# Delta rule scan: Grams of keys copied to SBUF once per chunk, kept in DRAM and loaded for the second visit

## The chip, the core and the metric

The kernel runs on one core of one Trainium2 chip. The metric is the device time of one execution in microseconds (us). The core has TensorE (PE, with its weight loads PEld), VectorE (DVE), ScalarE (ACT), GpSimd (POOL) and SyncE (SP), which here issues the DMAs. Matmuls write PSUM, eight banks of 128 x 512 fp32; the other operands are in SBUF.

## The reference

The program computes two transformer blocks on 512 tokens of width 1024, all in fp32: differential attention, a gated delta rule in both directions, an expert-choice feed-forward of 16 experts, and then a second block. The change touches the delta rule of the first block, which has 8 heads with keys and values of width 128 and runs once over the tokens and once over the reversed tokens. In each chunk, with keys k, a log decay g and a step beta, it needs (shortened):

```
k_beta = k * beta
a_mat  = where(strict, einsum('id,jd->ij', k_beta, k) * decay, 0)   # the Gram of keys, weighted
sol    = triangular_solve(a_mat + I, [v * beta, k_beta * exp(g)])
qk     = where(incl, einsum('id,jd->ij', q, k) * decay, 0)
# over the chunks:
v_new = u - w @ state
o     = q_dec @ state + qk @ v_new
state = state * g_last + k_dec.T @ v_new
```

The Gram of keys, k k^T of one chunk and head, depends on the keys alone. The decay and beta with which it is weighted are those of the direction.

## The kernel before

The stage works with chunks of 128 tokens (NT = 4 chunks) and walks through eight *positions*: `PAIRS[n] = (s, hg)`, step s = 0 to 3, and group of heads hg = 0 or 1. At a position both directions work at once, each on four heads: direction d = 0 on chunk s, direction d = 1 on chunk 3 - s. So a chunk that one direction meets in steps 0 and 1 is met by the other in steps 3 and 2: each Gram of keys is needed twice, once at positions 0 to 3 and once at positions 4 to 7. A position takes some 27 to 30 us.

The order of work on each engine is written out by hand: each engine has a loop over n with helper functions, and they meet by semaphores. While TensorE solves position n and runs the scan of n - 1, the others prepare n + 1. What matters for the change, by function and line of the profile:

- `gram_k` (L1246, TensorE): for each direction four matmuls 128 x 128 into the bank `bank(d, 1)`. In the trace an fp32 matmul shows as two records. In the loop it stands between `widest_P` (L1302) and `widest_X` (L1310) of the position before. `gram_q` (L1255) does the same for queries.
- `exponents` (L1591, L1592, VectorE), `decays` (L1427, L1432, ScalarE) and `keys` (L1487, GpSimd) make the factor BR of decay, mask and beta.
- `products` (VectorE): AT = Gram x BR, two instructions on L1598, then two on L1601 for the queries. Behind them stands `diagonal`: four small transposes on L1619 and one on L1611 (the semaphore `xop`).
- `level_P` (L1268, TensorE): the first matmuls of position n. They need AT of both directions and `xop`. Before the first position they need the inverses of 32 x 32 blocks too, which VectorE solves (L1651, L1653), and which go through DRAM: three stores to yrow (L1180) and four loads X32 (L1189).
- `corner` (L1643), `joined_T` (L1635), `outputs` (L1563), `states` (L1575) and `right` (L1584, L1586) are VectorE's other work in a position; `scan_ks` (L1327), `scan_v` (L1339), `scan_o` (L1349, L1351), `scan_s` (L1359) are TensorE's; L1219 is a filler, a projection of 8 matmuls 128 x 512 put where TensorE would wait, and ScalarE takes each out of PSUM (L1422).
- SyncE's one queue issues in its written order: pieces of weights for the fillers (L1157, 512 KB each, waiting until the filler two before is done), broadcast rows (L1166, L1173) and the transfers of inverses.

The place AT of direction d is the last but one (d = 0) or last (d = 1) eighth of the slab SL[2]; the scratch `sub` of the block solve is the same memory as AT of d = 1.

Of the kernel before, what the change touches and what calls it, by code (L numbers as in the profile page):

```python
# [13 lines left out]
F32 = mybir.dt.float32  # L14
ALU = mybir.AluOpType
# [3 lines left out]
P = 128  # L19
# [91 lines left out]
def build(nc, io):  # L111
    ctx = ExitStack()
    counts = {}
    with ctx:
# [5 lines left out]
        def sem(name):  # L120

            return cleared.pop(0) if cleared else ctx.enter_context(nc.semaphore(name))
# [667 lines left out]
        with nc.Block() as block:  # L790
# [200 lines left out]
            def _(dve):  # L991
# [28 lines left out]
                for p in range(NC3 + 1):  # L1020
# [46 lines left out]
        OG = SL[3][:, :]  # L1067
        ogT = OG.rearrange("p (h s) -> p h s", h=HEADS)
        names = ("zero", "lt_ready", "y_ready", "y_out", "x32", "xd_act", "xd_dve", "xop", "x64",
                 "gk_done", "gq_done", "row_read", "diff_ready", "qe_ready", "dec_ready", "ba_ready", "qd_ready", "AT_ready", "qk_ready",  # L1070
                 "P_done", "P_ready", "XO_done", "XO_ready", "XOT_done", "XOT_ready", "wP_done", "wP_ready", "XX_done", "XL_ready",
                 "ks_done", "bv_ready", "rr_ready", "vn_done", "vn_ready", "vs_ready", "o_done", "s_done",
                 "o_ready", "S_ready", "qq4", "sq4", "ss4", "rstd4", "og_ready", "ex_done", "ex_out", "ex_dve")
        E4 = {n: sem("d_" + n) for n in names}
        row_in = [sem(f"row_in{d}") for d in range(2)]
        brow_in = [sem(f"brow_in{d}") for d in range(2)]
        PAIRS = [(s, hg) for s in range(NT) for hg in range(2)]

        def all4(ap):
# [49 lines left out]
        def goes_on(n):  # L1129

            return PAIRS[n][0] < NT - 1

        def fresh(n):

# [8 lines left out]
        with nc.Block() as block:  # L1143
            @block.sync
            def _(sp):
# [48 lines left out]
                for m in range(3, KD + 2):  # L1194
                    load_piece(m)
                    if m in (5, 7, 8):
                        inverses_out((5, 7, 8).index(m))
                inverses_in()
                for m in range(KD, KD + AHEAD):
                    load_piece(m + 2)  # L1200
                rows(1)
                for n in range(len(PAIRS)):
                    if 1 <= n < len(PAIRS) - 1:
                        rows(n + 1)
                    for i in range(2):
                        m = extra(n, i)
                        if m is not None and m + 2 < len(EXTRA):
                            load_piece(m + 2)
                sp.wait_ge(E4["s_done"], 2 * (len(PAIRS) - 2))
                load_slab(sp, 7, w_in[:, GATE_G:GATE_G + 512], 512)  # L1210

            @block.tensor
            def _(pe):
# [26 lines left out]
                def gram_k(n):  # L1240
                    for q, d, c, heads, B, W in each(n):
                        if n:
                            pe.wait_ge(E4["AT_ready"], q - 1)
                        for i, h in enumerate(heads):
                            kc = gk[:, h, c * P:(c + 1) * P]
                            m = pe.matmul(part(bank(d, 1), i), kc, kc, start=True, stop=True)  # L1246
                        m.then_inc(E4["gk_done"], 1)
# [121 lines left out]
                for n in range(len(PAIRS) + 1):  # L1369
                    now, scan, ahead = n < len(PAIRS), n >= 1, n + 1 < len(PAIRS)  # L1370
                    if scan:
                        scan_ks(n - 1)
                    if now:
                        level_P(n)
                    if ahead:
                        gram_q(n + 1)
                    if now:
                        level_X(n)
                    if scan and now:
                        scan_v(n - 1)  # L1380
                    more(n, 0)
                    if now:
                        level_XT(n)
                    if scan and not now:
                        scan_v(n - 1)
                    if scan:
                        scan_o(n - 1)
                    if now:
                        widest_P(n)
                    if ahead:  # L1390
                        gram_k(n + 1)
                    if now:
                        widest_X(n)
                    if scan and goes_on(n - 1):
                        scan_s(n - 1)
                    more(n, 1)

            @block.scalar
            def _(act):
# [24 lines left out]
                def decays(n):  # L1424
# [5 lines left out]
                    for q, d, c, heads, B, W in each(n):  # L1430
                        act.wait_ge(E4["o_done"], q - 3)
                        a(cp(W["QD"], B["RW"], ACT.Exp), E4["dec_ready"])  # L1432

                def diagonal(n):

                    for q, d, c, heads, B, W in each(n):
# [17 lines left out]
                for m in range(1, KD - 1):  # L1454
                    attended(m)
                decays(0)
                attended(KD - 1)
                diagonal(0)
                filled(KD)
                for n in range(len(PAIRS) + 1):  # L1460
# [11 lines left out]
                        a(cp(flat(PMw), PS[0][:, 0:256], ACT.Copy), E4["wP_ready"])  # L1472
                    if ahead:
                        decays(n + 1)
                        diagonal(n + 1)
                    more(n, 1)

# [59 lines left out]
            def _(dve):  # L1537
# [56 lines left out]
                def products(n):  # L1594
                    for q, d, c, heads, B, W in each(n):
                        dve.wait_ge(E4["ba_ready"], q + 1)
                        dve.wait_ge(E4["gk_done"], q + 1)
                        v(tt(B["AT"], f4(bank(d, 1)[:, :]), B["BR"], ALU.mult), E4["AT_ready"])  # L1598
                    for q, d, c, heads, B, W in each(n):
                        dve.wait_ge(E4["gq_done"], q + 1)  # L1600
                        v(tt(W["QK"], f4(bank(d, 2)[:, :]), W["QK"], ALU.mult), E4["qk_ready"])  # L1601
# [181 lines left out]
            def expert_slab(eng, r):  # L1783
# [18 lines left out]
                for k in range(4):  # L1802
# [1 line left out]
                    slab_n[4 + k] += 16  # L1804
                    quarter_in.append((slab_in[4 + k], slab_n[4 + k]))

            spent.extend([inv["fac"], inv["rows"], inv["kt"], *piece_in, first_done, *row_in, *brow_in,
                          *[E4[n] for n in E4 if n not in ("qq4", "sq4", "ss4", "rstd4", "og_ready")]])
            @block.sync
            def _(sp):  # L1810
# [1588 lines left out]
```

## Time and profile before

| | us |
|---|---|
| runs, median (lowest to highest of 3) | 2232.25 (2231.83 to 2233.06) |
| profiled execution, its own time | 2233.42 |
| its span, first to last instruction | 2231.5 |
| TensorE busy | 2074.7 (93%) |
| VectorE busy | 905.9 (41%) |
| ScalarE busy | 484.1 (22%) |
| GpSimd busy | 230.2 (10%) |
| DMA moved | 499.98 MB |
| the stage of the change | from 463 to 755 in the span |

The span is what the trace shows; the execution's own time has 1.9 us more around it. An engine's share of busy time is a mean over stages with different limits, so each stage is read by itself. Columns of a timeline are the start in the span, the duration, the engine, the line, the operation, what it writes and reads, and in brackets how long the engine stood idle before and what ended that.

### The profile page before, as it was taken

What the parts mean: (1) busy time and instruction counts of PE and PEld (TensorE: products, weight loads), DVE (VectorE), ACT (ScalarE), POOL (GpSimd) and SP (SyncE); (2) the same over time, 40 slices, a digit from 0 to 9 for tenths busy, and PEclk for the clock granted to TensorE, in tenths of its full rate; (3) what the DMA queues carried; (4) which work ended last, traced back from release to release, by engine and by line L of the source; (5) the groups of instructions that cost most, each with busy time, mean ns of one, the idle gap of its engine ahead of it and who ended that gap; (6) DMA issues with size and microseconds to landing.
All of it is one profiled execution on the core that took longest, in us unless ns stands there. A gap on an engine that the chain in (4) does not pass through costs nothing.

```text
span 2231.5 us, 25322 instructions
## 1 busy us (share of the span) xinstructions
PE 2074.7 (93%) x10317; PEld 1130.4 (51%) x10317; DVE 905.9 (41%) x1507; ACT 484.1 (22%) x884; POOL 230.2 (10%) x163
## 2 busy tenths in 40 slices
PE   8999999998999999799999898989898978999998
PEld 5885564445666786443333333333332325865444
DVE  2447757783566653401110110101010104796964
ACT  2445645421222410100000000000000002332323
POOL 1320000301334030000000000000000003222000
PEclk9999999999999999899999999999999999999999
DMA  7220110024322334299999999999999996211111
GB/s 261 76 91 26 38 38 21 23 83 109 89 61 90 127 114 198 114 371 427 429 428 427 428 427 428 427 428 428 427 427 428 429 428 246 97 60 49 70 57 38
DMA packets 112789, 499.98 MB, mean 224 GB/s; under 512 B 23525, under 2 KB 51203, under 8 KB 87459
## 3 DMA queue, kind: packets, MB, share of 16 engines
q1 hardware_dynamic: 112675, 498.38, 55.8%
q8 instruction: 82, 1.34, 0.2%
q14 instruction: 32, 0.26, 0.0%
HBM read 493.31 MB, written 5.05 MB: 223 GB/s over the span
## 4 chain that ended last, share of the span: by engine, by line
PE 55%; DMA 19%; DVE 2%; ACT 1%; issue 1%; SPq 0%; DVEq 0%; ACTq 0%
PE PS L2059 8%; PE PS L2030 8%; DMA SL<-w_up 8%; PE PS L1219 7%; DMA R<-w_up 6%; PE PS L1919 4%; PE PS L2763 4%; PE PS L2740 3%; DMA SL<-w_down 3%; PE PS L1943 2%; PE PS L2004 2%; DMA SL<-w_gate 2%; PE PS L2759 1%; PE PS L3230 1%; PE PS L3224 1%; PE PS L2097 1%
## 5 line engine op out<-in xcount | busy, mean ns | idle before, releaser
L2030 PE MATMUL PS<-R 128*64 128x512 f32 x1024 | 230.4, 597 | 33.1 <-DMA R<-w_up 24.1
L2030 PE MATMUL PS<-SL,R 128*64 128x512 f32 x1024 | 227.2, 595 | 26.2 <-DMA SL<-w_gate 18.7
L2344 DVE TENSOR_TENSOR HT<-HT,PS 128x512 f32<-128x512 f32 x32 | 20.6, 684 | 365.2 <-PE PS L2030 365.2
L2030 PEld LDWEIGHTS PS<-SL,R 128*64 128x64 f32 x1024 | 72.5, 137 | 178.2 <-issue 128.2
L2030 PEld LDWEIGHTS PS<-R 128*64 128x64 f32 x1024 | 69.9, 137 | 182.1 <-issue 125.7
L2349 DVE COPY HT<-PS 64x512 f32<-64x512 f32 x16 | 10.9, 683 | 304.0 <-PE PS L2060 304.0
L2059 PE MATMUL PS<-SL,HT 128*64 128x512 f32 x256 | 114.5, 594 | 13.5 <-ACT HT L2174 6.2
L2059 PE MATMUL PS<-R,HT 128*64 128x512 f32 x256 | 114.3, 594 | 12.5 <-ACT HT L2174 7.0
L865 PE MATMUL PS<-HT,SL 128*128 128x512 f32 x256 | 115.0, 603 | 0.8 <-PEq L282 0.8
L2060 PE MATMUL PS<-SL,HT 128*64 128x512 f32 x256 | 115.0, 596 | 0.0
L2060 PE MATMUL PS<-R,HT 128*64 128x512 f32 x256 | 114.8, 595 | 0.0
L1219 PE MATMUL PS<-HT,X 128*128 128x512 f32 x256 | 113.5, 595 | 0.0
L2169 ACT ACTIVATE HT<-PS 128x512 f32<-128x512 f32 x32 | 17.4, 594 | 418.6 <-PE PS L2030 418.6
L2507 POOL MEMSET SL<- 128x2048 f32 x1 | 1.8, 1805 | 1022.0 <-PE PS L2060 1022.0
L2763 PE MATMUL PS<-HT,SL 128*128 128x512 f32 x192 | 84.7, 596 | 0.0
L865 PEld LDWEIGHTS PS<-HT,SL 128*128 128x128 f32 x256 | 48.9, 194 | 59.4 <-issue 59.4
L1219 PEld LDWEIGHTS PS<-HT,X 128*128 128x128 f32 x256 | 47.7, 192 | 53.4 <-issue 53.2
L2059 PEld LDWEIGHTS PS<-SL,HT 128*64 128x64 f32 x256 | 33.4, 137 | 75.7 <-issue 70.0
L2059 PEld LDWEIGHTS PS<-R,HT 128*64 128x64 f32 x256 | 33.7, 137 | 73.1 <-issue 71.0
L2160 ACT ACTIVATE R<-PS 128x512 f32<-128x512 f32 x14 | 8.4, 597 | 268.8 <-PE PS L2004 268.8
L2097 PE MATMUL PS<-HT,R 128*128 128x512 f32 x112 | 53.9, 619 | 10.4 <-DVE HT L2350 10.4
L625 PE MATMUL PS<-HT,SL 128*128 128x512 f32 x128 | 61.3, 612 | 0.0
(484 smaller groups left out, 3524.8 us busy)
## 6 DMA issues: line engine op xcount, KB each, us to landing
R<-w_gate SPq DMA_DIRECT2D x32, 2048.0 KB, 35.4
SL<-w_gate SPq DMA_DIRECT2D x32, 2048.0 KB, 33.6
SL<-w_up SPq DMA_DIRECT2D x32, 2048.0 KB, 32.7
R<-w_up SPq DMA_DIRECT2D x32, 2048.0 KB, 33.0
SL<-w_down SPq DMA_DIRECT2D x31, 2048.0 KB, 35.4
R<-w_down SPq DMA_DIRECT2D x28, 2048.0 KB, 27.8
SL<-w_in SPq DMA_DIRECT2D x18, 2048.0 KB, 8.0
SL<-grow SPq DMA_DIRECT2D x32, 256.0 KB, 4.6
```

Source lines behind the costliest of these rows:

```text
L625: m = pe.matmul(PS[5][:, :], slab(2 + f // 4)[:, k, f % 4 * P:(f % 4 + 1) * P], hT[:, k, :], start=(k == 0), stop=(k == KD - 1))
L865: m = pe.matmul(PS[n % 4][:, :], slab(i)[:, k, j * P:(j + 1) * P], hT[:, k, :], start=(k == 0), stop=(k == KD - 1))
L1219: m_ = pe.matmul(to[:, :], piece[m % 2][:, k, :], src[:, k, :], start=(k == 0), stop=(k == KD - 1))
L1919: m = pe.matmul(bank_[:, g, :], w[:, k, g * P:(g + 1) * P], x_[:, k, :], start=((aside or p in OPENS) and g == k == 0), stop=(k == K2 - 1) ...
L1943: m = pe.matmul(PS[u % 4][:, :], mT[:, k, t * P:(t + 1) * P], slab(slot)[:, k, :], start=(k == 0), stop=(k == KD - 1))
L2004: m = pe.matmul(OB[hf][:, c * P:(c + 1) * P], h2[:, t, 256 * j + k:256 * (j + 1):2], Sel[q % 2][:, t, :], start=(t == 0), stop=(t == NT - 1))
L2030: m = pe.matmul(banks[n][half * CAP:(half + 1) * CAP, :], XC[x // 2 % 2][:, 2 * j + k, toks], w[:, k, (2 * half + n) * 512:(2 * half + n + ...
L2059: pe.matmul(DB[0:CAP, :], hk, w[:, k, 0:512], start=first, stop=last)
L2060: m = pe.matmul(DB[CAP:P, :], hk, w[:, k, 512:1024], start=first, stop=last)
L2097: pe.matmul(OB[half][:, :], STc[:, t, :], YP[:, half * 512:(half + 1) * 512], start=True, stop=True)\
L2740: m = pe.matmul(zbank(i, p)[:, g, :], w[:, k, g * P:(g + 1) * P], x_[:, k, :], start=(p in OPENS and g == k == 0), stop=(k == K2 - 1), ski ...
L2763: m = pe.matmul(bank_[:, :], slab(i % 2)[:, k, j * P:(j + 1) * P], hT[:, k, :], start=(k == 0), stop=(k == KD - 1))
```

## The change

At positions 0 to 3 ScalarE copies the Gram from PSUM into the place AT (`evict_gram`), SyncE stores AT into a DRAM tensor `gramk` (`keep_gram`, one store of 256 KB for each direction), and VectorE multiplies AT by BR in place, once the store has landed (the semaphores `gk_kept0` and `gk_kept1`), since the multiply overwrites what is stored. At positions 4 to 7 no Gram is computed. SyncE loads it from `gramk` into AT (`known_gram`) once `widest_P` of the position before has read the old AT, and VectorE multiplies in place once the load has landed. `KNOWN` is 4. The tensor is indexed by the chunk and the group of heads, so the second visit finds what the other direction stored.

```diff
--- before.py
+++ after.py
@@ -1067,13 +1067,15 @@
         OG = SL[3][:, :]
         ogT = OG.rearrange("p (h s) -> p h s", h=HEADS)
         names = ("zero", "lt_ready", "y_ready", "y_out", "x32", "xd_act", "xd_dve", "xop", "x64",
-                 "gk_done", "gq_done", "row_read", "diff_ready", "qe_ready", "dec_ready", "ba_ready", "qd_ready", "AT_ready", "qk_ready",
+                 "gk_done", "gk_out", "gk_kept0", "gk_kept1", "gq_done", "row_read", "diff_ready", "qe_ready", "dec_ready", "ba_ready", "qd_ready", "AT_ready", "qk_ready",
                  "P_done", "P_ready", "XO_done", "XO_ready", "XOT_done", "XOT_ready", "wP_done", "wP_ready", "XX_done", "XL_ready",
                  "ks_done", "bv_ready", "rr_ready", "vn_done", "vn_ready", "vs_ready", "o_done", "s_done",
                  "o_ready", "S_ready", "qq4", "sq4", "ss4", "rstd4", "og_ready", "ex_done", "ex_out", "ex_dve")
         E4 = {n: sem("d_" + n) for n in names}
         row_in = [sem(f"row_in{d}") for d in range(2)]
         brow_in = [sem(f"brow_in{d}") for d in range(2)]
+        gramk_in = [sem(f"gramk_in{d}") for d in range(2)]
+        gramk = nc.dram_tensor("gramk", [2 * NT, P, 512], F32, kind="Internal").ap()
         PAIRS = [(s, hg) for s in range(NT) for hg in range(2)]
 
         def all4(ap):
@@ -1129,6 +1131,13 @@
         def goes_on(n):
 
             return PAIRS[n][0] < NT - 1
+
+        KNOWN = len(PAIRS) // 2
+
+        def gramk_at(n, d):
+
+            s, hg = PAIRS[n]
+            return gramk[2 * chunk(s, d) + hg]
 
         def fresh(n):
 
@@ -1196,8 +1205,21 @@
                     if m in (5, 7, 8):
                         inverses_out((5, 7, 8).index(m))
                 inverses_in()
+                for q, d, c, heads, B, W in each(0):
+                    sp.wait_ge(E4["gk_out"], q + 1)
+                    sp.dma_start(gramk_at(0, d), flat(B["AT"])).then_inc(E4[f"gk_kept{d}"], 16)
                 for m in range(KD, KD + AHEAD):
                     load_piece(m + 2)
+                def keep_gram(n):
+                    for q, d, c, heads, B, W in each(n):
+                        sp.wait_ge(E4["gk_out"], q + 1)
+                        sp.dma_start(gramk_at(n, d), flat(B["AT"])).then_inc(E4[f"gk_kept{d}"], 16)
+
+                def known_gram(n):
+                    sp.wait_ge(E4["wP_done"], n)
+                    for q, d, c, heads, B, W in each(n):
+                        sp.dma_start(flat(B["AT"]), gramk_at(n, d)).then_inc(gramk_in[d], 16)
+
                 rows(1)
                 for n in range(len(PAIRS)):
                     if 1 <= n < len(PAIRS) - 1:
@@ -1206,6 +1228,10 @@
                         m = extra(n, i)
                         if m is not None and m + 2 < len(EXTRA):
                             load_piece(m + 2)
+                        if i == 0 and n + 1 < KNOWN:
+                            keep_gram(n + 1)
+                        elif i == 0 and n + 1 < len(PAIRS):
+                            known_gram(n + 1)
                 sp.wait_ge(E4["s_done"], 2 * (len(PAIRS) - 2))
                 load_slab(sp, 7, w_in[:, GATE_G:GATE_G + 512], 512)
 
@@ -1240,7 +1266,7 @@
                 def gram_k(n):
                     for q, d, c, heads, B, W in each(n):
                         if n:
-                            pe.wait_ge(E4["AT_ready"], q - 1)
+                            pe.wait_ge(E4["gk_out"], q - 1)
                         for i, h in enumerate(heads):
                             kc = gk[:, h, c * P:(c + 1) * P]
                             m = pe.matmul(part(bank(d, 1), i), kc, kc, start=True, stop=True)
@@ -1387,7 +1413,7 @@
                         scan_o(n - 1)
                     if now:
                         widest_P(n)
-                    if ahead:
+                    if n + 1 < KNOWN:
                         gram_k(n + 1)
                     if now:
                         widest_X(n)
@@ -1430,6 +1456,14 @@
                     for q, d, c, heads, B, W in each(n):
                         act.wait_ge(E4["o_done"], q - 3)
                         a(cp(W["QD"], B["RW"], ACT.Exp), E4["dec_ready"])
+
+                def evict_gram(n):
+
+                    if n == 0:
+                        act.wait_ge(E4["y_ready"], len(FINAL))
+                    for q, d, c, heads, B, W in each(n):
+                        act.wait_ge(E4["gk_done"], q + 1)
+                        a(cp(flat(B["AT"]), bank(d, 1)[:, :], ACT.Copy), E4["gk_out"])
 
                 def diagonal(n):
 
@@ -1454,6 +1488,7 @@
                 for m in range(1, KD - 1):
                     attended(m)
                 decays(0)
+                evict_gram(0)
                 attended(KD - 1)
                 diagonal(0)
                 filled(KD)
@@ -1472,6 +1507,8 @@
                         a(cp(flat(PMw), PS[0][:, 0:256], ACT.Copy), E4["wP_ready"])
                     if ahead:
                         decays(n + 1)
+                        if n + 1 < KNOWN:
+                            evict_gram(n + 1)
                         diagonal(n + 1)
                     more(n, 1)
 
@@ -1594,8 +1631,11 @@
                 def products(n):
                     for q, d, c, heads, B, W in each(n):
                         dve.wait_ge(E4["ba_ready"], q + 1)
-                        dve.wait_ge(E4["gk_done"], q + 1)
-                        v(tt(B["AT"], f4(bank(d, 1)[:, :]), B["BR"], ALU.mult), E4["AT_ready"])
+                        if n < KNOWN:
+                            dve.wait_ge(E4[f"gk_kept{d}"], 16 * (n + 1))
+                        else:
+                            dve.wait_ge(gramk_in[d], 16 * (n - KNOWN + 1))
+                        v(tt(B["AT"], B["AT"], B["BR"], ALU.mult), E4["AT_ready"])
                     for q, d, c, heads, B, W in each(n):
                         dve.wait_ge(E4["gq_done"], q + 1)
                         v(tt(W["QK"], f4(bank(d, 2)[:, :]), W["QK"], ALU.mult), E4["qk_ready"])
```

On ScalarE, at the preparation of position 2, the rows before are these (L1452 takes v out of PSUM, L1422 a filler, L1472 belongs to the widest level, L1427 and L1432 are `decays`, L1444 is its share of `diagonal`):

```order
L1452 ACTIVATE SL<-PS 128x512 x2
L1422 ACTIVATE R<-PS 128x512
L1472 ACTIVATE SL<-PS 128x256
L1427 ACTIVATE SL<-SL 128x512 x2
L1432 ACTIVATE SL<-SL 128x512 x2
L1444 ACTIVATE SL<-R 32x4x32 x4
L1422 ACTIVATE R<-PS 128x512
```

And after the change, where L1466 is the copy of the Gram:

```order
L1486 ACTIVATE SL<-PS 128x512 x2
L1448 ACTIVATE R<-PS 128x512
L1507 ACTIVATE SL<-PS 128x256
L1453 ACTIVATE SL<-SL 128x512 x2
L1458 ACTIVATE SL<-SL 128x512 x2
L1466 ACTIVATE SL<-PS 128x512 x2
L1478 ACTIVATE SL<-R 32x4x32 x4
L1448 ACTIVATE R<-PS 128x512
```

The two copies stand behind the exponentials and ahead of the diagonal; nothing else has moved.

In SyncE's queue, from the last store of inverses to the rows of position 2, there stood before (X<-w_in is a piece, SL<-grow the broadcast rows):

```order
L1180 DMA yrow<-SL 256x1x256
L1157 DMA X<-w_in 128x8x128
L1189 DMA R<-yrow 32x64x32 x4
L1157 DMA X<-w_in 128x8x128
L1166 DMA SL<-grow 128x512 x2
L1173 DMA SL<-grow 128x512 x2
L1157 DMA X<-w_in 128x8x128 x2
L1166 DMA SL<-grow 128x512 x2
```

Now there stands:

```order
L1189 DMA yrow<-SL 256x1x256
L1166 DMA X<-w_in 128x8x128
L1198 DMA R<-yrow 32x64x32 x4
L1210 DMA gramk<-SL 128x512 x2
L1166 DMA X<-w_in 128x8x128
L1175 DMA SL<-grow 128x512 x2
L1182 DMA SL<-grow 128x512 x2
L1166 DMA X<-w_in 128x8x128
L1216 DMA gramk<-SL 128x512 x2
L1166 DMA X<-w_in 128x8x128
L1175 DMA SL<-grow 128x512 x2
```

The stores of position 0 come behind the four loads of the inverses, and those of position 1 between the two pieces of an iteration.

On TensorE, behind the last scan_o matmuls of position 2, while position 4 is prepared, the rows before were:

```order
L1302 MATMUL PS<-SL 64x64 x8
L1246 MATMUL PS<-R 128x128 x8
L1310 MATMUL PS<-SL 64x64 x8
L1359 MATMUL PS<-SL,R 128x128 x8
L1219 MATMUL PS<-HT,X 128x512 x8
L1327 MATMUL PS<-X,R 128x128 x8
```

And now:

```order
L1328 MATMUL PS<-SL 64x64 x8
L1336 MATMUL PS<-SL 64x64 x8
L1385 MATMUL PS<-SL,R 128x128 x8
L1245 MATMUL PS<-HT,X 128x512 x8
L1353 MATMUL PS<-X,R 128x128 x8
```

The Gram, L1246 before, is gone between the two widest levels; the same holds for positions 5 to 7.

## Rows read from the trace of the kernel before

**Rows 1.** The page's engines: busy us, share of the span, instructions.

```profile
PE 2074.7 (93%) x10317; PEld 1130.4 (51%) x10317; DVE 905.9 (41%) x1507; ACT 484.1 (22%) x884; POOL 230.2 (10%) x163
```

**Rows 2.** Chain of waits, 440 to 800 us: start us, us, engine, written tile, line.

```profile
541.71 3.71 PE PS L1246 x16
...
654.59 1.98 PE PS L1246 x16
...
709.81 0.70 DVE SL L1565
...
721.71 0.32 DVE SL L1611
```

**Rows 3.** Timeline of VectorE, positions 0 to 2: start, us, instruction, idle before.

```profile
524.54 1.31 DVE L1619 STREAM_TRANSPOSE SL<-R 32x128 f32<-32x128 f32 x4 [10.31 <-DMA R<-yrow]
...
546.59 0.88 DVE L1643 TENSOR_SCALAR SL<-PS 64x256 f32<-64x256 f32 x2 [3.15 <-PE PS L1310]
...
574.92 1.42 DVE L1598 TENSOR_TENSOR SL<-PS,SL 128x512 f32<-128x512 f32 x2
...
579.29 0.31 DVE L1611 STREAM_TRANSPOSE SL<-R 128x128 f32<-128x128 f32 x1 [0.15 <-DVE SL L1619]
```

**Rows 4.** Timeline of VectorE, positions 3 and 5.

```profile
605.70 0.31 DVE L1611 STREAM_TRANSPOSE SL<-R 128x128 f32<-128x128 f32 x1
...
661.70 1.42 DVE L1598 TENSOR_TENSOR SL<-PS,SL 128x512 f32<-128x512 f32 x2
...
665.94 0.31 DVE L1611 STREAM_TRANSPOSE SL<-R 128x128 f32<-128x128 f32 x1
```

**Rows 5.** Timeline of ScalarE, position 2: the row behind the exponentials.

```profile
574.60 1.32 ACT L1444 ACTIVATE SL<-R 32x128 f32<-32x128 f32 x4
```

**Rows 6.** Groups by line, 526 to 756 us: busy us, mean ns, idle before.

```profile
L1592 DVE TENSOR_TENSOR SL<-SL,wab 128x512 f32<-128x512 f32 x14 | 9.7, 692 | 0.5
...
L1598 DVE TENSOR_TENSOR SL<-PS,SL 128x512 f32<-128x512 f32 x14 | 9.7, 691 | 0.5
...
L1452 ACT ACTIVATE SL<-PS 128x512 f32<-128x512 f32 x16 | 9.6, 597 | 25.2 <-PE PS L1339 25.2
```

**Rows 7.** Timeline of TensorE: first matmuls of positions, and widest_P of 0.

```profile
526.31 0.22 PE L1268 MATMUL PS<-R,SL 32*32 32x32 f32 x2 [4.68 <-DVE SL L1611]
...
540.59 1.12 PE L1302 MATMUL PS<-SL 64*64 64x64 f32 x16 [2.45 <-DVE SL L1635]
...
553.74 0.22 PE L1268 MATMUL PS<-R,SL 32*32 32x32 f32 x2
...
580.28 0.22 PE L1268 MATMUL PS<-R,SL 32*32 32x32 f32 x2
...
608.59 0.22 PE L1268 MATMUL PS<-R,SL 32*32 32x32 f32 x2
...
667.75 0.22 PE L1268 MATMUL PS<-R,SL 32*32 32x32 f32 x2
...
722.16 0.22 PE L1268 MATMUL PS<-R,SL 32*32 32x32 f32 x2 [2.06 <-DVE SL L1611]
```

**Rows 8.** Timeline of the SyncE queue: issue of the four loads of inverses.

```profile
515.27 6.26 SPq L1189 DMA_DIRECT2D R<-yrow  x4
```

**Rows 9.** DMA issues of the span: count, KB each, median us to landing.

```profile
SL<-grow SPq DMA_DIRECT2D x32, 256.0 KB, 4.6
...
y<-X SPq DMA_DIRECT2D x8, 256.0 KB, 2.0
...
R<-scratch SPq DMA_DIRECT2D x4, 256.0 KB, 8.4
...
yrow<-SL SPq DMA_DIRECT2D x2, 256.0 KB, 4.4
```

**Rows 10.** Stretches: length, busy us of PE, PEld, DVE, ACT, POOL; PEclk, DMA share, GB/s.

```profile
540.20:547.00 6.80, 6.41 (x49) 5.85 (x50) 3.48 (x7) 2.87 (x7) 2.84 (x2) 0.50 0.13 40
724.50:728.00 3.50, 3.50 (x17) 3.35 (x17) 1.96 (x4) 0.60 (x1) 1.92 (x2) 0.51 0.76 276
```

More of the change, by code:

```diff
@@ L1805, in expert_slab @@
                     quarter_in.append((slab_in[4 + k], slab_n[4 + k]))
-            spent.extend([inv["fac"], inv["rows"], inv["kt"], *piece_in, first_done, *row_in, *brow_in,
+            spent.extend([inv["fac"], inv["rows"], inv["kt"], *piece_in, first_done, *row_in, *brow_in, *gramk_in,
                           *[E4[n] for n in E4 if n not in ("qq4", "sq4", "ss4", "rstd4", "og_ready")]])
```

## The prediction

> **What bounds the kernel now.** I read four views. First the page's table of engines: TensorE is busy 93% of the span, so only what shortens or stalls TensorE moves the time [rows 1]. Then the chain of waits, in the stage of the change (463 to 755 us). It runs through TensorE nearly everywhere, and a Gram of keys is a link of it: sixteen matmul records (two per fp32 matmul) in 1.98 us; at position 1, with TensorE at half clock, 3.71 us. Only at the stage's start and at position 7 does the chain leave TensorE, for VectorE [rows 2]. Third, the timelines of the engines at the positions: from them I take how long before TensorE needs its operand the other engines have it. Last, the clock by stretches: after TensorE idled before 540.6 and before 722.2, it was granted 0.50 of 2.4 GHz, the lower of its two levels, for some microseconds [rows 7, 10].
>
> The condition for TensorE's first matmuls of a position (line 1268, "level_P") is that VectorE has written AT (line 1598) and, behind that in its own order, the QK products and the transposes up to line 1611. I call the distance from the end of 1611 to the start of 1268 the slack.
>
> **Removed: Grams of positions 4 to 7 on TensorE.** Four times sixteen records of 1.98 us is 7.9 us of work. What is late next is VectorE. At position 5 the chain of VectorE ends at 665.94 + 0.31 = 666.25 and level_P starts at 667.75 [rows 4, 7]: slack 1.50, of which about 0.13 is the hand-over (VectorE done at 721.71 + 0.32 = 722.03, TensorE on at 722.16) [rows 2, 7]. So the removal pays 1.50 - 0.13 = 1.4 us there, not 1.98; positions 4 and 6 repeat the pattern 29.6 us before and behind, three in all. At position 7 VectorE is on the chain already, from 709.81 to 722.03 [rows 2], and nothing upstream of it ends earlier: 0. Sum **-4.2 us** (3 x 1.4); bounds 0 (something new is late) and -7.9 (all four pay in full).
>
> **The loads that take their place.** Two of 256 KB are issued when widest_P of the position before is done, at 654.6 for position 5 [rows 2], and products wants them at 661.70 [rows 4]: 7.1 us. Two 256 KB broadcasts landed in 4.6 us, the stores to y in 2.0, the slowest rows of that size in 8.4 [rows 9]. What stands behind the wait (the next piece, the rows) is wanted a good filler later. I take 0; at 8.4 it would be 1.3 us at each of four positions, 5.2 in all.
>
> **The multiply reads SBUF in place of PSUM.** Line 1598, from PSUM, takes 691 ns; line 1592, the same shape from SBUF alone, 692 [rows 6]: 0. The Trainium skill (Perfetto Trace Analysis, Optimizing Scalar/DVE Operations) gives VectorE about 60 ns of access overhead on SBUF and about 125 on PSUM; by it each pair would be 0.13 us shorter, some 0.8 us over the six positions where VectorE ends last. The rows disagree, and they decide.
>
> **Added: the copy and the store, positions 0 to 3.** Per position two ScalarE copies of 597 ns (line 1452 is the same copy) [rows 6] behind `decays`, and two stores of 256 KB, on whose landing the AT product now waits. The nearest row is the store to y: 128 partitions by 512 floats, on a quiet queue, 2.0 us from issue. The stores to yrow took 4.4, each issued right behind a 512 KB piece [rows 9]; at positions 1 to 3 the last piece is issued some 10 us ahead, so I take 2.05 with the semaphore, bounds 2.0 and 4.4. By the Trainium skill (DMA: Bandwidth & Descriptors, Anatomy of one DMA) a DMA costs about 2.0 us plus bytes over 436 GB/s, for 256 KB an estimate of 2.6, and a completion that must reach HBM can be slow; that would add 0.6 at position 2 and about 0.4 at 3.
>
> *Position 0.* The store stands in SyncE's order behind the four loads of the inverses (issued until 515.27 + 6.26 = 521.53 [rows 8]), which land at 524.5 [rows 3]. So the two stores are issued at 521.6 and 522 and queue behind them; I let them land at 526.0 and 526.8. VectorE was done with the products at 524.54 - 10.31 = 514.2, in the shadow of these loads [rows 3]. Now: AT at 526.1 to 527.6, two QK products (1.45) to 529.05, four transposes (1.35) to 530.4, the last one to 530.7; level_P at 530.8 in place of 526.31 [rows 7]: **+4.5 us**. Bounds: both landed with the loads, 2.9 (four products of 0.725); 4.4 after 524.5, 7.5.
>
> *Position 1.* ScalarE copies the second Gram only when it is made, 541.71 + 3.71 = 545.4 [rows 2]; copy to 546.05, store landed at 548.2. VectorE is free of `corner` at 546.59 + 0.88 = 547.5 [rows 3], does the first product, then the second at 548.25: **0**. With 4.4 us of landing it would end 2.4 us late against a slack of about 1.6 to level_P at 553.74 [rows 7], +0.8.
>
> *Position 2.* `decays` ends at 574.57, where diagonal starts (574.60 [rows 5]). Copies to 575.2 and 575.83, stores issued 575.27 and 575.9, landed 577.35 and 578.0. VectorE stood ready at 574.92 [rows 3]. So AT ends 578.8 in place of 576.34, and 1611 ends at 579.60 + 2.4 = 582.0; level_P at 582.1 in place of 580.28 [rows 7]: **+1.8 us** (4.4 us of landing: +4.2). What waits behind the product on VectorE is the QK products, transposes and the gate's merge; for these, only TensorE.
>
> *Position 3.* The same 2.4 us later: 606.01 + 2.4 = 608.4 against 608.59, since scan_ks stands ahead of level_P there [rows 4, 7]: **0** (4.4: +2.3). `right`, behind it on VectorE, moves by less than one instruction of 0.7, and scan_v, which begins with the other direction's half, covers that.
>
> **The sum.** +4.5 + 0 + 1.8 + 0 - 4.2 = **+2.1 us** on the profiled execution: its span 2231.5 to 2233.6, its time 2233.4 to 2235.5. The median of the runs lies 1.2 below the profiled one; I predict the median as 2232.25 + 2.1 = **2234.4 us**.
>
> **The clock.** Rows show half clock for 3.5 and 6.8 us, behind idles of 2.06 and 2.45 [rows 7, 10], each worth half its length (the Gram at 541.71 lost 3.71 - 1.98 = 1.7 by itself). With an earlier or later start the stretch at 540 may not recur (-3.4 at best); a TensorE idle of 1.8 at position 2 may bring one (+1.7), and so may the longer idle at position 7 (4.0 in place of 2.06; +1.7). I take 0 and keep -3.4 and +3.4.
>
> **Rivals.**
> *B, late stores (slower).* The stores land as those to yrow do, 4.4. For: same issuer, same kind of target; against: no piece just ahead of them. 2.1 + 2.4 (position 0) + 0.8 + 2.4 + 2.3 = +10.0, and two more idles long enough for the clock, +3.4: 2245.7. It decides from a landing above about 2.3 us at position 2.
> *C, the clock (slower).* The stall at 2 and the longer idle at 7 bring half clock: +2.1 + 3.4 = +5.5, 2237.8. For: an idle of 2.06 did so before 722.2; against: 1.8 is shorter than any that did.
> *D, Grams pay in full (faster).* If VectorE were not late next, all four save 1.98 (-7.9), the stores at 0 land with the loads (+2.9), and the idle at 2 vanishes because the clock stays up at 1 and re-times it: -5.0, 2227.2. Against: VectorE's slack of 1.50 at position 5 is under 1.98 [rows 4, 7].
> *E, late loads.* 5.2 late, so the gain is gone: +2.1 + 5.2 = +7.3, 2239.6. Against: 7.1 us of room.
>
> **How the numbers follow.** A change of under 0.2%, 4.5 us, can hardly be told from none here. Forecast 0.62, B 0.13, C 0.13, D 0.06, E 0.06. Forecast alone spans -1.3 to +5.5 (its clock half used): of its 0.62 I give 0.02 to slower. Faster 0.07 (D and a lucky clock), slower 0.27 (part of C stays within), same 0.66. Range 2230.0 to 2240.0: it leaves out B and D.
>
> **What the profile after would show.** Right: level_P of position 0 released by VectorE some 4.5 us later than the inverses allow; VectorE idle about 2.4 us ahead of the first product at positions 2 and 3, with DMA as releaser; TensorE idle 1.8 at position 2 and about 0.6 at 4 to 6; gramk stores landing in about 2, loads under 5. Wrong: a landing over 3 us for the stores of positions 1 to 3, VectorE waiting for a gramk load, or stages outside 463 to 755 us that changed their length.

## The result, and the profile after

The changed kernel takes 2245.45 us, median of 4 runs (2244.66 to 2247.66); the kernel before, beside it on the same chip, took 2232.65 (2231.83 to 2234.31, 4 runs). The ratio is 1.0058, interval 1.0045 to 1.0071: slower by 12.8 us, where I had forecast 2.1, which "can hardly be told from none". It lies outside my range. The number is rival B's (2245.7), but B is not the reason: the stores landed in time.

The page after, engines, as in [rows 1] (busy us, share, instructions):

```profile
PE 2068.8 (92%) x10253; PEld 1124.3 (50%) x10253; DVE 914.7 (41%) x1507; ACT 488.9 (22%) x892; POOL 235.9 (11%) x163
```

TensorE has 64 records less and is busy 5.9 us less, so the four Grams are gone. VectorE is busy 8.8 us more with the same 1507 instructions, and GpSimd 5.7 us more with its 163. No instruction was added to either; some of them got longer. That is the first thing to see, and no view of waits shows it.

The DMA issues of the page after, as in [rows 9]:

```profile
gramk<-SL SPq DMA_DIRECT2D x8, 256.0 KB, 2.1
SL<-gramk SPq DMA_DIRECT2D x8, 256.0 KB, 2.9
```

The stores landed in 2.1 us (I had 2.05), the loads in 2.9 (I had under 5): B and E fall here.

VectorE by line, 526 to 770 us, as in [rows 6] (busy us, mean ns of one, idle before):

```profile
L1629 DVE TENSOR_TENSOR SL<-SL,wab 128x512 f32<-128x512 f32 x14 | 9.7, 692 | 0.5
...
L1638 DVE TENSOR_TENSOR SL<-SL 128x512 f32<-128x512 f32 x14 | 18.3, 1307 | 7.6 <-DMA gramk<-SL 7.2
```

Line 1638 is the AT product, 1598 before. It took 691 ns an instruction; now it takes 1307 in the mean, 8.6 us more in all, with its 7.2 us of waiting for stores beside that. Line 1629, which was 1592 and was my yardstick for a multiply that reads SBUF alone, is still at 692.

VectorE's timeline after, at positions 0 to 5, as in [rows 3, 4] (start, us, instruction, idle before it):

```profile
522.62 1.45 DVE L1638 TENSOR_TENSOR SL<-SL 128x512 f32<-128x512 f32 x2 [21.46 <-DMA gramk<-SL]
...
547.86 1.42 DVE L1638 TENSOR_TENSOR SL<-SL 128x512 f32<-128x512 f32 x2 [2.16 <-DMA gramk<-SL]
...
576.21 2.31 DVE L1638 TENSOR_TENSOR SL<-SL 128x512 f32<-128x512 f32 x2 [2.49 <-DMA gramk<-SL]
...
607.03 2.25 DVE L1638 TENSOR_TENSOR SL<-SL 128x512 f32<-128x512 f32 x2 [2.56 <-DMA gramk<-SL]
...
636.10 3.16 DVE L1638 TENSOR_TENSOR SL<-SL 128x512 f32<-128x512 f32 x2
...
667.69 3.15 DVE L1638 TENSOR_TENSOR SL<-SL 128x512 f32<-128x512 f32 x2
...
673.67 0.31 DVE L1651 STREAM_TRANSPOSE SL<-R 128x128 f32<-128x128 f32 x1
```

The idles ahead of positions 2 and 3 are the forecast's (2.4 expected; 2.49 and 2.56 here). The durations are not: a pair is 1.42 at position 1, 2.31 at 2, 2.25 at 3, 3.09 to 3.16 from 4 on. What else runs beside them? GpSimd's timeline after, position 5:

```profile
663.08 3.07 POOL L1524 TENSOR_TENSOR SL<-SL 128x512 f32<-128x512 f32 x2 [12.02 <-ACT SL L1453]
666.23 2.62 POOL L1531 TENSOR_TENSOR SL<-SL,R 128x512 f32<-128x512 f32 x2
668.92 2.82 POOL L1537 TENSOR_TENSOR SL<-R,small 128x512 f32<-128x512 f32 x2
```

and the same place of the kernel before:

```profile
660.24 2.62 POOL L1494 TENSOR_TENSOR SL<-SL,R 128x512 f32<-128x512 f32 x2
662.93 2.16 POOL L1500 TENSOR_TENSOR SL<-R,small 128x512 f32<-128x512 f32 x2
```

GpSimd multiplies the queries (lines 1494 before, 1531 after) and the values (1500, 1537) beside VectorE's products, before and after. Before, each product took one operand from PSUM, and both engines ran at their own pace (1.42 for the pair, 2.16 for GpSimd's values). After, both operands of the AT product are in SBUF: the pair takes 3.15 and GpSimd's values 2.82. The queries' pair, which had begun before the product, kept its 2.62. At positions 0 and 1 no such GpSimd work lies beside the product, and it takes 1.45 and 1.42.

TensorE after, as in [rows 7] (lines 1294 level_P, 1328 widest_P, 1336 widest_X, 1272 the Gram of keys, 1281 that of queries):

```profile
527.31 0.26 PE L1294 MATMUL PS<-R,SL 32*32 32x32 f32 x2 [8.53 <-DVE SL L1651]
...
542.04 2.05 PE L1272 MATMUL PS<-R 128*128 128x128 f32 x16
...
552.57 0.22 PE L1294 MATMUL PS<-R,SL 32*32 32x32 f32 x2 [0.80 <-DVE SL L1651]
...
581.93 0.26 PE L1294 MATMUL PS<-R,SL 32*32 32x32 f32 x2 [2.75 <-DVE SL L1651]
...
642.55 0.22 PE L1294 MATMUL PS<-R,SL 32*32 32x32 f32 x2 [1.70 <-DVE SL L1651]
642.94 3.66 PE L1281 MATMUL PS<-R 128*128 128x128 f32 x16
...
661.13 0.68 PE L1336 MATMUL PS<-SL 64*64 64x64 f32 x16 [0.54 <-ACT SL L1507]
...
730.63 0.26 PE L1294 MATMUL PS<-R,SL 32*32 32x32 f32 x2 [5.12 <-DVE SL L1651]
```

From position 2 on TensorE idles ahead of level_P for VectorE: 2.75 us at 2 (I had 1.8), 0.85 at 3 (I had none), 1.70 and 1.69 at 4 to 6 where I had 0.6, 5.12 at 7 (I had 4.0). The clock by stretches after, as in [rows 10]:

```profile
580.00:584.00 4.00, 2.07 (x39) 2.03 (x40) 2.21 (x6) 0.28 (x1) 1.58 (x4) 0.71 0.93 276
642.00:646.00 4.00, 3.45 (x47) 3.44 (x48) 3.79 (x7) 0.28 (x1) 1.14 (x4) 0.64 0.88 296
728.50:739.00 10.50, 7.57 (x68) 5.86 (x69) 6.12 (x13) 1.47 (x3) 3.23 (x6) 0.52 0.40 144
```

Three idles of 2.75, 1.70 and 5.12 us are followed by stretches granted in part 0.5 of 2.4 GHz, the lower level (the first two windows hold some of either level). Line 1281, the Gram of queries, shows the price: 3.26 us behind position 2 and 3.66 behind position 4, against 2.05 behind 1, 3, 5 and 6. On the other side the half-clock stretch at 540 did not recur (the Gram at 542.04 took 2.05, not 3.71).

To place the loss, here are the distances in us from the stage's first filler matmul (462.88 before, 460.03 after) to the first matmul of each position, and to the first one of the next block:

| | 0 | 1 | 2 | 3 | 4 | 5 | 6 | 7 | next block |
|---|---|---|---|---|---|---|---|---|---|
| before | 63.4 | 90.9 | 117.4 | 145.7 | 175.3 | 204.9 | 234.5 | 259.3 | 292.2 |
| after | 67.3 | 92.5 | 121.9 | 152.5 | 182.5 | 214.1 | 244.1 | 270.6 | 304.7 |
| each step's change | +3.9 | -2.2 | +2.8 | +2.3 | +0.4 | +2.0 | +0.4 | +1.7 | +1.1 |
| I had | +4.5 | 0 | +1.8 | 0 | -1.4 | -1.4 | -1.4 | 0 | 0 |

The stage is 12.5 us longer: the loss of 12.8 lies in it.

### The profile page after: what moved, and what is told of

Same layout as the page of the kernel before. It is cut to its first block and busy times, and to the rows that moved or that the text cites. A ratio compares the mean times of both kernels' runs of the same rounds, so it can differ in the third digit from the quotient of the medians.

```text
span 2242.7 us, 25231 instructions
## 1 busy us (share of the span) xinstructions
PE 2068.8 (92%) x10253; PEld 1124.3 (50%) x10253; DVE 914.7 (41%) x1507; ACT 488.9 (22%) x892; POOL 235.9 (11%) x163
## 5 line engine op out<-in xcount | busy, mean ns | idle before, releaser
L2099 PE MATMUL PS<-R,HT 128*64 128x512 f32 x256 | 114.3, 594 | 12.5 <-ACT HT L2214 7.0
```

The costliest lines, as they stand in the source:

```text
L2099: pe.matmul(DB[0:CAP, :], hk, w[:, k, 0:512], start=first, stop=last)
```

## Experiments

Theory P: a VectorE multiply with both operands in SBUF is held up while GpSimd works in SBUF. Its rivals: S, the waits for the stores are the whole loss; D, the new DMA traffic slows VectorE's accesses; M, the multiply is slow by itself, for the place of its operand (a Gram copied or loaded to SBUF, read and written in place). Ratios are against the kernel before, in runs beside it; "held" means above 1.42 for a pair.

**e1_pool_waits.** The changed kernel, in which GpSimd waits for both AT products between its keys and its queries:

```diff
                     if ahead:
                         keys(n + 1)
+                        pool.wait_ge(E4["AT_ready"], 2 * n + 4)
                         queries(n + 1)
```

> The changed kernel, with one wait more: GpSimd begins the queries of a position only when VectorE has written AT. Theory P (port): the AT multiply, which now reads both inputs from SBUF, is held while GpSimd works in SBUF. Then the pairs on the AT line, 2.3 us at positions 2 and 3 and 3.16 us at 4 to 7 in the changed kernel, fall to 1.42, and the time falls from 2245.5 by 6 to 8 us, to 2237.5 to 2239.5. Rival theory M (the multiply itself): reading and writing the same place, or a place just filled by a DMA, is slow by itself: the pairs stay at 3.1 us and the time at 2245.5, or above by what the wait costs.

Measured: 2235.94 us (10 runs), ratio 1.0013 (1.0004 to 1.0023), 9.5 us under the changed kernel. Its rows by line, and VectorE's and GpSimd's timelines at position 5:

```profile
L1639 DVE TENSOR_TENSOR SL<-SL 128x512 f32<-128x512 f32 x14 | 9.7, 692 | 6.0 <-DMA gramk<-SL 5.6
```

```profile
664.37 1.42 DVE L1639 TENSOR_TENSOR SL<-SL 128x512 f32<-128x512 f32 x2
```

```profile
665.91 2.63 POOL L1531 TENSOR_TENSOR SL<-SL,R 128x512 f32<-128x512 f32 x2 [3.07 <-DVE SL L1639]
668.62 2.16 POOL L1537 TENSOR_TENSOR SL<-R,small 128x512 f32<-128x512 f32 x2
```

The product is back at 692 ns, GpSimd's line 1537 at 2.16. GpSimd's wait of 3.07 costs little: its work now lies beside `right`, another multiply from SBUF alone, whose first instruction takes 0.90 to 0.92 in place of 0.69 at positions 4 to 7. Operand, stores and loads are as they were. P holds and M falls, and S is not the whole loss. The waits for stores, 5.6 us, still stand here, and the first matmuls of position 2 show what they do without any held product (line 1281 is the Gram of queries):

```profile
582.06 0.22 PE L1294 MATMUL PS<-R,SL 32*32 32x32 f32 x2 [1.88 <-DVE SL L1652]
582.45 2.97 PE L1281 MATMUL PS<-R 128*128 128x128 f32 x16
```

TensorE idles 1.88 us, the 1.8 of the forecast, and then falls to the lower clock (granted 0.50 of 2.4 GHz at 584 to 586).

**e2_copy_beside.** The changed kernel, in which at positions 0 to 3 ScalarE copies the Gram to free places of the output buffer and the stores leave from there, while the product reads PSUM:

```diff
-                        a(cp(flat(B["AT"]), bank(d, 1)[:, :], ACT.Copy), E4["gk_out"])
+                        a(cp(kept(n, d), bank(d, 1)[:, :].rearrange("p (h n) -> p h n", h=4), ACT.Copy), E4["gk_out"])
...
                         if n < KNOWN:
-                            dve.wait_ge(E4[f"gk_kept{d}"], 16 * (n + 1))
+                            dve.wait_ge(E4["gk_out"], q + 1)
+                            v(tt(B["AT"], f4(bank(d, 1)[:, :]), B["BR"], ALU.mult), E4["AT_ready"])
```

> The changed kernel, with the copies of positions 0 to 3 put beside AT (into the part of the output buffer that is written only from position 2's outputs on), and the multiply reading PSUM as before, behind the copy. No store is waited for in products; positions 4 to 7 are as changed. Theory S (the store wait costs what the trace shows up to the first matmuls of position 3, 6.8 us against before in the stage's own time): 2245.5 - 6.5 = 2239. If the waits on stores were hidden by others (rival: the same loss comes back through TensorE's clock or ScalarE), 2243 or more.

Measured: 2238.04 us, ratio 1.0024 (1.0014 to 1.0033), 7.4 under the changed kernel. At positions 4 to 7, where it still loads and multiplies in SBUF, the pair is held, and at positions 0 to 3, where it reads PSUM, it is not, though GpSimd works beside it at 2 and 3. Positions 2 and 5:

```profile
573.40 1.42 DVE L1645 TENSOR_TENSOR SL<-PS,SL 128x512 f32<-128x512 f32 x2 [0.45 <-ACT SL L1472]
...
660.49 3.15 DVE L1648 TENSOR_TENSOR SL<-SL 128x512 f32<-128x512 f32 x2
```

So the loss has two parts. e1 takes away the held product at all positions; e2 takes away the waits for stores, and with them the held pairs of positions 2 and 3.

**e3_both.** Both edits together.

> Both edits together. By P and S the losses are separate and add: 2245.5 - 7 - 6.5, and the saving that was predicted for the missing Grams is left: about 2230 to 2232, at or a little under the kernel before (2232.65). By M with S: 2239 (only the stores' part is won). If it falls clearly below 2230, the removal of the Grams paid more than 1.4 us each at positions 4 to 6.

Measured: 2230.70 us, ratio 0.9994 (0.9985 to 1.0003), no difference from before. The stage is 290.1 us, 2.1 under before. Taken away first, the held product is worth 9.5 us (changed kernel to e1); what e2 leaves of it, the pairs at positions 4 to 7, is worth 7.3 (e2 to e3). e2's edit is worth 7.4, and the waits for stores alone 5.2 (e1 to e3). The 2 us between the two ways are what both edits take away, the pairs at 2 and 3 (0.89 and 0.83 us too long in the changed kernel). These are differences of medians whose ratios are known to 0.1%, 2 us. The stages of the traces, one execution each, are 304.7 (changed kernel), 297.0 (e1), 294.8 (e2) and 290.1 (e3): 7.7 or 4.7 for the product, 9.9 or 6.9 for the waits. Both parts are there by either measure; which is the larger isn't shown.

**e4_no_gram.** The kernel before with the Grams of positions 4 to 7 left out and nothing in their place: the products there multiply what an earlier position left in the bank, so this computes something else. VectorE's wait for these Grams is left out too (not shown).

```diff
-                    if ahead:
+                    if n + 1 < len(PAIRS) // 2:
                         gram_k(n + 1)
```

> The kernel before with the Grams of positions 4 to 7 left out: products read what an earlier position left in the bank, so the output isn't the reference's. It shows what the removal is worth without any copy, store or load. My step (VectorE is late next, 1.4 us at three positions): 2232.65 - 4.2 = 2228.4. Rival (TensorE's time is saved in full at all four): 2224.7. Rival (the Gram covered something else, such as ScalarE's copy between the two widest levels, so less is left): 2230 or more.

Measured: 2228.39 us, ratio 0.9980 (0.9970 to 0.9989), -4.2 as forecast. The steps to positions 4, 5 and 6 take 28.2 us each, before 29.6; the step to 7 takes 24.9, before 24.8. VectorE's last transpose and TensorE's level_P of position 5, and TensorE at widest_X before it:

```profile
663.07 0.31 DVE L1612 STREAM_TRANSPOSE SL<-R 128x128 f32<-128x128 f32 x1
```

```profile
652.26 0.68 PE L1310 MATMUL PS<-SL 64*64 64x64 f32 x16 [0.54 <-ACT SL L1472]
...
663.52 0.22 PE L1268 MATMUL PS<-R,SL 32*32 32x32 f32 x2
```

VectorE ends at 663.38 and TensorE starts at 663.52, the hand-over of 0.14: VectorE is late next, as I had it. And 0.54 of the 1.98 us has a second taker. The Gram stood between widest_P and widest_X and covered ScalarE's copy; with it gone TensorE idles there. By either account some 1.4 us are left.

**e5_copied.** The kernel before, with one thing alone: at positions 4 to 7 ScalarE copies the Gram from PSUM to AT's place, and the product reads SBUF. No store or load is added. Of the edit, the part on VectorE:

```diff
+                        if n >= 4:
+                            dve.wait_ge(E4["gk_out"], q + 1 - 8)
+                            v(tt(B["AT"], B["AT"], B["BR"], ALU.mult), E4["AT_ready"])
+                            continue
                         v(tt(B["AT"], f4(bank(d, 1)[:, :]), B["BR"], ALU.mult), E4["AT_ready"])
```

> The kernel before, all Grams computed, no gramk and no DMA more; at positions 4 to 7 ScalarE copies the Gram into AT and VectorE multiplies there in place, from SBUF alone. Theory P (the second SBUF input is held while GpSimd works): the pairs take 3.1 us as in the changed kernel. The slack of 1.5 at positions 4 to 6 covers most of the 1.7 more, position 7 pays it: about +0.4 x 3 + 1.7 = +2.9, with TensorE's clock up to +4.6: 2235.5 to 2237.3. Rival D (what holds the multiply is that its operand has just come by DMA, or the traffic of the loads): pairs 1.42 and 2232.6.

Measured: 2235.24 us, ratio 1.0012 (1.0003 to 1.0021). By line, and GpSimd's timeline at position 5:

```profile
L1608 DVE TENSOR_TENSOR SL<-SL 128x512 f32<-128x512 f32 x8 | 12.5, 1568 | 0.3
```

```profile
657.80 2.62 POOL L1502 TENSOR_TENSOR SL<-SL,R 128x512 f32<-128x512 f32 x2
660.50 2.82 POOL L1508 TENSOR_TENSOR SL<-R,small 128x512 f32<-128x512 f32 x2
```

1568 ns and 2.82 us again, with no Gram traffic at all: D falls. With the Gram still on TensorE, TensorE waits for VectorE only 0.34, 0.69 and 0.33 us at positions 4, 5 and 6, where the changed kernel waits 1.70, 1.69 and 1.69; so it costs 2.8 us here and not 7 to 9 (expected 2.9 or more; the time came out 0.3 under the range).

**e6_store_first.** e1 with position 0's stores issued ahead of the loads of the inverses:

```diff
+                    if m == 8:
+                        for q, d, c, heads, B, W in each(0):
+                            sp.wait_ge(E4["gk_out"], q + 1)
+                            sp.dma_start(gramk_at(0, d), flat(B["AT"])).then_inc(E4[f"gk_kept{d}"], 16)
                 inverses_in()
-                for q, d, c, heads, B, W in each(0):
...
```

> The kernel of e1_pool_waits, with position 0's two stores issued ahead of the four loads of the inverses, where the Gram has been copied some 3 us earlier. Theory S for position 0: the products are then done in the shadow of the loads, and level_P of position 0 starts where it did before: 2235.9 - 3.9 = 2232. Rival: the stores push the piece and the inverses back in the queue, or the shorter idle of TensorE changes its clock, and less than 2 us are won.

Measured: 2232.90 us, ratio 1.0002 (0.9992 to 1.0011). That is 3.0 under e1, where 3.9 was expected. Position 0 starts 63.6 us into the stage, before 63.4: the 3.9 us there came from the stores' place in SyncE's order. VectorE:

```profile
512.89 2.42 DVE L1640 TENSOR_TENSOR SL<-SL 128x512 f32<-128x512 f32 x2 [9.42 <-DMA gramk<-SL]
```

Moved earlier, the first product falls beside GpSimd's work and is held (2.42); in the shadow of the loads that costs nothing.

**e7_reordered and e8_before_reordered.** If VectorE is late next, its order is the lever. e7 is e3 with the diagonal's transposes, which level_P waits for, ahead of the query products, which it does not need; e8 is the kernel before with the same edit.

```diff
                         products(n + 1)
                         diagonal(n + 1)
+                        query_products(n + 1)
```

> The kernel of e3_both; on VectorE the transposes of `diagonal` go ahead of the two products for the queries, which nobody wants before the next position's scan. If VectorE is what TensorE waits for at the first matmuls, its chain ends 1.45 us earlier: 1.45 at position 7, and about 0.5 at each of 4 to 6, so that the Grams pay in full there: 2230.7 - 3.0 = 2227.7. Rival: the products for the queries are late for scan_o or the gate's merge, and nothing is won.

> The kernel before with the same reordering on VectorE and nothing else. Positions 1 to 6 have slack anyway; at position 0 nothing (the products are done long before) and at 7 level_P comes 1.45 us earlier: 2232.65 - 1.5 = 2231.2. Rival: nothing, 2232.6.

Measured: e7 2229.71 us, ratio 0.9991 (0.9981 to 1.0000), 1.0 under e3 and not 3; e8 2233.01, ratio 1.0002 (0.9992 to 1.0012), nothing. In e7 level_P of position 7 waits 1.93 us where e3 waits 3.38. In e8 it starts 1.1 us sooner, but the next block at 292.3 as ever. The row that explains both is scan_v behind it, before and in e8:

```profile
724.25 3.80 PE L1339 MATMUL PS<-SL 128*128 128x128 f32 x16 [0.73 <-DVE SL L1586]
```

```profile
722.04 3.47 PE L1339 MATMUL PS<-SL 128*128 128x128 f32 x16 [2.18 <-DVE SL L1586]
```

Line 1586 is `right`, which stands on VectorE behind the two query products wherever these are put, so its chain to `right` is no shorter: scan_v starts 261.4 us into the stage before and 261.7 in e8. What level_P gains, scan_v waits (2.18 for 0.73). It is the same in e7 (2.40, in e3 0.90). The stage of e7 is 288.6 against 290.1 in e3, but 1.0 of these 1.5 us lies in the step to position 1, where the lower clock comes and goes (see the clock, below).

**e9_kept_busy and e10_reordered_again.** e9 is e7 with 34 small matmuls whose results nobody reads, in TensorE's idles at positions 0 and 7, to see what the lower clock costs; e10 is e7 again, beside it.

```diff
                 def level_P(n):
+                    if n == 0:
+                        keep_busy(PS[7], 18)
+                    elif n == len(PAIRS) - 1:
+                        keep_busy(PS[5], 7)
```

> The kernel of e7_reordered; where TensorE stands idle at positions 0 (twice) and 7 it does 18, 9 and 7 matmuls 128 x 128 into a bank that nobody uses, so that it is busy though nothing is computed. Theory C (the clock's share): the half-clock stretches behind these idles, which in the stage of e7 last some 10 us together, go, worth half of that at most: 2229.7 - 3 to 5 = 2225 to 2227. Rival: the added matmuls delay the first matmuls behind them or the clock falls elsewhere, and the time stays within 1 us of e7.

> The kernel of e7_reordered unchanged, in more rounds, to see whether it lies below the kernel before. From the traces (stage 288.6 against 292.2 us) it should be 2232.5 - 3.7 = 2228.8; if the gain is lost outside the stage, 2232.

Measured: e9 2227.96 us (12 runs), ratio 0.9978 (0.9969 to 0.9988); e10 2230.18 (11 runs), ratio 0.9989 (0.9980 to 0.9997). The medians differ by 2.2 us, and eleven of e9's twelve runs lie under e10's median, so e9 is likely the faster; but the stages of the two profiled executions are equally long (287.4 and 287.2). So the gain of e9 is not shown to come from the stage, and what the lower clock costs isn't settled by it. The changed plan, mended by e1's wait, e2's copy and e7's order, beats the kernel before by 0.1% (e10; e7's interval just reaches 1.0000).

## Why the prediction was wrong

**The step that failed** is the one headed "The multiply reads SBUF in place of PSUM", which I priced at 0. I compared line 1598 (691 ns, from PSUM) with line 1592 (692, from SBUF) [rows 6] and took the two places for equal. They are, for a VectorE that runs alone. But line 1592 stands where GpSimd is idle or only then starts (at position 5 its last row starts at 656.99, and GpSimd's first at 657.08), and the AT product stands where GpSimd runs its queries and values. With both operands in SBUF the pair took 3.15 in place of 1.42 (1.7 more at each of positions 4 to 7, 0.89 and 0.83 at 2 and 3). With the waits and half-clock stretches that this brought, it was worth 7.3 us for positions 4 to 7 (e2 to e3) and 9.5 for all (changed kernel to e1), and e5 shows it with no part of the change but ScalarE's copy and the multiply from SBUF. e1 is the plan with every term that I priced and without the held product: it takes 2235.94 us, and I had forecast 2234.4. The rule for it is in the Trainium skill (SBUF — State Buffer, section "SBUF: two separate sides"): VectorE and GpSimd share a pair of ports that is locked for a whole instruction, and a VectorE instruction with two SBUF inputs contends for it with a GpSimd instruction that reads SBUF. The trace agrees: both engines were longer (3.15 for 1.42, 2.82 for 2.16), and neither was when one operand came from PSUM. I had weighed the Trainium skill's figures for the access overhead on either memory and not this rule, which spoke against the change.

The trace of before had a hint, too: one instruction of line 1586, a multiply of two SBUF operands, at 724.95, beside GpSimd at 724.34, took 0.98 us where its eleven others took 0.69:

```profile
724.95 0.98 DVE L1586 TENSOR_TENSOR SL<-SL 128x512 f32<-128x512 f32 x1
```

```profile
724.34 1.04 POOL L1500 TENSOR_TENSOR SL<-R,small 128x512 f32<-128x512 f32 x1 [0.83 <-DVE SL L1586]
```

I had left its group's mean, 715 in place of 692, unread.

**Removed Grams, -4.2: right.** e4 gives -4.2, at the three positions that I named, and 0 at position 7. In the changed kernel none of it is seen: where each should save 1.4, the held pair makes VectorE 1.73 later.

**Loads, 0: right.** They landed in 2.9 us, and no product waited for one.

**Stores, 2.05: right.** 2.1 us. The estimate of 2.6 that stands beside it in the prediction was too long for these stores.

*Position 0, +4.5:* +3.9, and e6 shows that it is the place in SyncE's order. *Position 1, 0:* the product waited 2.16 for the store and TensorE 0.80 for VectorE, which I did not have, but the step came out at -2.2, because the lower clock's stretch at 540 did not recur. That was my "-3.4 at best", and it was luck, as the next item shows. *Position 2, +1.8:* +2.8, which is the wait as forecast and 0.89 of a held product. *Position 3, 0:* +2.3. The wait of 2.56 alone was covered, as I had it: in e1 VectorE waits 2.59 there and TensorE not at all. But the step starts with the lower clock behind position 2's idle, 1.6 us in e1 too, and with 0.83 held TensorE waited 0.85 more.

**The clock, 0 with 3.4 to either side: too low at position 2.** One stretch went (at 540), two came, behind 2 (line 1281 at 3.26 against 2.05, 1.2 us) and behind 4 (3.66, 1.6 us), and the one behind 7 grew. Behind 2 rival C was right with its +1.7: in e1 and e6, where nothing is held there, TensorE idles 1.88 and 1.87 us, the Gram of queries takes 2.97 and 3.58, and the step to position 3 is 1.6 and 1.7 us longer. The stretch behind 4 came with the held product only (2.05 in e1). The one at 540 belongs to the execution and not to the kernel: e7 and e10 are the same kernel, and the Gram of keys there took 3.08 us in one trace and 2.05 in the other.

**What adds up.** By the medians the held product is 9.5 and the waits alone 5.2, or, with positions 2 and 3 counted to the stores' edit, 7.3 and 7.4; that is 14.7, less the 1.9 by which e3 lies under before: 12.8. Of the Grams' -4.2 some 2.3 us (e3 to e4) are not there in e3. e3 has eight copies, stores and loads and GpSimd's wait more than e4; in the two traces 1.2 us of the difference lie in the stage, 0.9 of it behind level_P of position 7. Which of them it is stays open, and it is near what these runs can tell apart.

## What to carry to other kernels

Before an operand moves from PSUM to SBUF, look at what GpSimd does at that very moment, and take the duration from a row that has the same neighbours, not only the same shape. A held instruction shows as a longer duration and never as a wait, so compare busy times with equal counts first. Work removed from the busiest engine pays only up to the slack of the next one: here 1.4 of 1.98 us, at three places of four.

## What the runs showed of the hardware

- Two VectorE multiplies of 128x512 fp32 took 1.42 us alone, and 3.09 to 3.18 with both operands in SBUF beside GpSimd's multiplies (positions 4 to 7 of the changed kernel, e2 and e5); GpSimd's own pair went from 2.16 to 2.82. With one operand in PSUM neither changed. The loss was not equal: 1.73 us for VectorE, 0.66 for GpSimd.
- An idle of TensorE of 1.70 us ahead of 642.55 was followed by the lower clock (3.66 us for a Gram of 2.05). Idles of 1.69 ahead of 674.13 and 704.10 were not (the same Gram took 2.05, and the four microseconds from 674 and from 704 were granted 1.00), and neither was one of 2.04 in e2, ahead of 666.93. The length of the idle alone doesn't tell it in this kernel, and behind the idle of 2.45 us at position 0 the lower clock came in one execution of a kernel and not in another of the same (e7 granted 0.50 from 539 to 541, e10 granted 1.00 throughout; 3.08 and 2.05 us for the Gram behind it).
- A matmul group taken out between two dependent steps can uncover another engine's hand-over: 0.54 us ahead of widest_X in each kernel that has no Gram there.
